# A decoder layer on one Trainium2 core: seven of the 22 gate-and-up tile pairs computed as seven block products each

## The chip, the cores and the metric

One Trainium2 chip, one core of it. The metric is the time of one execution in device microseconds (us). In the profile PE is TensorE's matrix multiplication, PEld its loading of weights, DVE is VectorE, ACT ScalarE, POOL GpSimd and SP SyncE, which issues most DMAs.

## The reference

One decoder layer in float32 on x of 512 tokens by 1024 channels: a token mixer (three parallel mixers, merged with gates, then an output projection and a residual) and a feed-forward network. The change touches only the latter:

```
h = rms_norm(x, norm_pre_ffn)                                # 512 x 1024
f = (silu(h @ ffn_w_gate) * (h @ ffn_w_up)) @ ffn_w_down     # hidden width 2816 = 22 x 128
x = x + rms_norm(f, norm_post_ffn)
```

## The kernel before

**Split products.** A float32 product is made of three matmuls: each operand is split into a high part (rounded to fp32r) and a low part (the rest), and high by high, high by low and low by high are added in PSUM. For a weight tile ACT copies the raw tile in WRAW to WHI (`hi_part`, line 817) and POOL subtracts to get WLO (`lo_part`, line 703). h, transposed to channels by tokens, lies split in HHI and HLO as 8 chunks of 128 channels by 512 tokens.

**Gate and up.** The hidden width has 22 tiles of 128. Each has a gate tile and an up tile of weights (8 chunks of 128x128), so there are 44 tiles, numbered from FF0. They go by four: step i (0 to 10) does the tile pairs f = 0 and f = 1, and each tile is `ffn_tile` (line 2508): 8 chunks by 3 matmuls (lines 2010 to 2012) that stream 512 tokens into one PSUM bank. For a pair DVE then multiplies the gate by RINV, the rows' norm (`gate_of`, line 1800), ACT takes the sigmoid (line 1114), DVE multiplies twice (`gated`, line 1806; `hidden`, line 1815), and the result goes in two token halves of 256 into SA (f = 0) or SB (f = 1). `hidden_sums` (lines 1820 to 1825) forms four sums for the down projection, which is itself done as seven block products; ACT and DVE split them (`hidden_high`, line 1119; `hidden_low`, line 1831).

**Start of the stage.** The first two tiles are done in token halves (`first_half_tile`, lines 2496 to 2506: matmuls that stream 256 tokens). Then come tiles FF0+2 and FF0+3, which are the pair f = 1 of step 0, and from step 1 on a loop.

**Order and buffers.** Every engine works through its own list in order and waits on semaphores. WRAW has four places of a tile, loaded by SP; WHI and WLO have two places each, so a tile may be split once the tile two before it is done (`dense_done`). TensorE may begin a tile when its low part is there (`w_lo`), and a pair once the pair two before it was taken from PSUM (`ff_hid`). The banks of step i are psum 0 to 3; psum 4 to 7 are idle in the loop, and the down projection uses them after it. DVE's order in a step is gate_of(i, 0), hidden_low(i-1), gated, hidden, gate_of(i, 1), gated, hidden, hidden_sums(i).

## Time and profile before

| | us |
|---|---|
| median of 3 runs | 1006.49 (1006.16 to 1007.11) |
| the profiled execution | 1006.44 |
| its span, first to last instruction | 1004.3 |

| engine | busy us | share |
|---|---|---|
| PE | 986.6 | 98% |
| PEld | 792.5 | 79% |
| DVE | 669.1 | 67% |
| POOL | 471.7 | 47% |
| ACT | 400.6 | 40% |

The feed-forward network begins at about 650 us of the span; the part from tile FF0+2 on lies at 664.5 to 892.8 us, the down projection behind it. The granted TensorE clock was 1.00 of full speed throughout. An engine's busy time counts an instruction from its start to its end, waits for a port of the memory within it too; a matmul's own duration contains its pipeline, so the step from one matmul's start to the next's is what counts.

### The profile page before, as it was taken

The numbers are of one execution on the slowest core, as the hardware profiler recorded it, in microseconds if no ns is written. First come the engines' busy times: TensorE is split into PE (matmuls) and PEld (weight loads), VectorE is DVE, ScalarE is ACT, GpSimd is POOL, SyncE is SP. The second block draws the span as 40 slices with busy tenths as digits, with TensorE's granted clock in tenths as the row PEclk, the third lists the DMA queues.
The fourth block names the chain that finished last, engine by engine and source line by source line (L and its number), as shares of the span: only waits on it lengthen the run. The fifth ranks groups of instructions, "written<-read, shape, count | busy, mean of one in ns | idle before, by whom it ended". The sixth has DMA issues, their size and how long they took to land.

```text
span 1004.3 us, 19112 instructions
## 1 busy us (share of the span) xinstructions
PE 986.6 (98%) x7694; PEld 792.5 (79%) x7694; DVE 669.1 (67%) x1046; ACT 400.6 (40%) x761; POOL 471.7 (47%) x495
## 2 busy tenths in 40 slices
PE   6999999999999999999999999999999999999997
PEld 5787777777777777777778888888888888888886
DVE  3799786466566955556547881356665556689987
ACT  4134432321323335445556444542322322345563
POOL 3376557244335766756673447444444444420000
PEclk9999999999999999999999999999999999999999
DMA  9345533122224554213014647343333333345552
GB/s 262 88 130 155 114 95 65 24 66 64 66 66 114 157 152 126 65 33 85 22 58 128 193 127 247 89 147 86 102 93 95 105 88 100 94 125 179 158 164 108
DMA packets 149446, 111.31 MB, mean 111 GB/s; under 512 B 21189, under 2 KB 132047, under 8 KB 149368
## 3 DMA queue, kind: packets, MB, share of 16 engines
q1 hardware_dynamic: 145644, 104.16, 35.8%
q10 hardware_dynamic: 3692, 6.07, 2.2%
q8 instruction: 54, 0.88, 0.4%
q14 instruction: 24, 0.20, 0.1%
q0 software_dynamic: 32, 0.00, 0.0%
HBM read 99.70 MB, written 10.52 MB: 110 GB/s over the span
## 4 chain that ended last, share of the span: by engine, by line
PE 86%; DVE 10%; issue 1%; DMA 1%; POOL 1%; ACT 1%; SPq 0%; DVEq 0%; ACTq 0%
PE ps L2062 33%; PE ps L2010 8%; PE ps L2011 8%; PE ps L2012 8%; PE ps L2076 4%; PE ps L2180 3%; PE ps L2425 3%; PE ps L2543 2%; PE ps L2545 2%; PE ps L2544 2%; PE ps L2367 2%; DVE XF L1295 2%; PE ps L2450 1%; PE ps L2451 1%; PE ps L2449 1%
## 5 line engine op out<-in xcount | busy, mean ns | idle before, releaser
L703 POOL TENSOR_TENSOR WLO<-WRAW,WHI 128x1024 fp32r<-128x1024 f32 (+1 forms) x92 | 204.9, 2228 | 225.7 <-ACT WHI L817 225.6
L2062 PE MATMUL ps<-HLO,WHI 128*128 128x512 f32 x440 | 178.3, 405 | 0.0
L2062 PE MATMUL ps<-HHI,WHI 128*128 128x512 f32 x440 | 175.5, 399 | 1.0 <-DVE HLO L1327 0.7
L817 ACT ACTIVATE WHI<-WRAW 128x1024 fp32r<-128x1024 f32 (+1 forms) x91 | 85.9, 945 | 194.7 <-PE ps L2012 121.4
L2010 PE MATMUL ps<-HHI,WHI 128*128 128x512 f32 x336 | 131.1, 390 | 0.0
L2012 PE MATMUL ps<-HHI,WLO 128*128 128x512 f32 x336 | 130.7, 389 | 0.0
L2011 PE MATMUL ps<-HLO,WHI 128*128 128x512 f32 x336 | 130.7, 389 | 0.0
L2062 PE MATMUL ps<-HHI,WLO 128*128 128x512 f32 x440 | 118.0, 397 | 0.9 <-issue 0.9
L707 POOL CAST WHI<-WRAW 128x256 fp32r<-128x256 f32 (+1 forms) x133 | 62.8, 472 | 106.3 <-PE ps L2062 106.1
L738 POOL TENSOR_TENSOR WLO<-WRAW,WHI 128x256 fp32r<-128x256 f32 x132 | 105.6, 800 | 10.7
L2062 PEld LDWEIGHTS ps<-HHI,WHI 128*128 128x128 f32 x440 | 82.6, 188 | 23.0 <-issue 4.4
L2062 PEld LDWEIGHTS ps<-HLO,WHI 128*128 128x128 f32 x440 | 82.6, 188 | 22.7 <-issue 5.1
L2062 PEld LDWEIGHTS ps<-HHI,WLO 128*128 128x128 f32 x440 | 80.6, 188 | 19.2 <-issue 2.4
L2010 PEld LDWEIGHTS ps<-HHI,WHI 128*128 128x128 f32 x336 | 63.1, 188 | 13.3 <-issue 0.2
L2012 PEld LDWEIGHTS ps<-HHI,WLO 128*128 128x128 f32 x336 | 63.1, 188 | 13.2
L2011 PEld LDWEIGHTS ps<-HLO,WHI 128*128 128x128 f32 x336 | 63.1, 188 | 13.2 <-issue 0.2
L1002 ACT ACTIVATE EB<-EB,STAT 128x257 f32<-128x257 f32 (+5 forms) x96 | 50.4, 527 | 49.6 <-DVE STAT L1674 42.4
L1806 DVE TENSOR_TENSOR SQ<-SQ,FTG 128x512 f32<-128x512 f32 x22 | 55.0, 2499 | 11.2 <-ACT SQ L1114 11.2
L767 POOL TENSOR_SCALAR EB<-EB,STAT,GLT 128x128 f32<-128x128 f32 (+3 forms) x64 | 38.6, 615 | 29.3 <-DVE STAT L1690 29.1
L1800 DVE TENSOR_TENSOR FTG<-ps,RINV 128x512 f32<-128x512 f32 x22 | 15.2, 691 | 51.2 <-PE ps L2012 51.2
L1697 DVE COPY PTB<-ps 128x512 f32<-128x512 f32 (+3 forms) x36 | 20.6, 572 | 32.1 <-PE ps L2076 32.1
L1674 DVE CUSTOM_DVE_ANT_0 EB<-ps,TB 128x128 f32<-128x128 f32 (+3 forms) x64 | 28.2, 488 | 19.2 <-PE ps L2367 16.9
(452 smaller groups left out, 2001.7 us busy)
## 6 DMA issues: line engine op xcount, KB each, us to landing
WRAW<-in_w_in SPq DMA_DIRECT2D x47, 512.0 KB, 4.2
WRAW<-in_w_gate SPq DMA_DIRECT2D x22, 512.0 KB, 3.9
WRAW<-in_w_up SPq DMA_DIRECT2D x22, 512.0 KB, 3.9
WRAW<-in_w_down SPq DMA_DIRECT2D x19, 512.0 KB, 3.8
spilled<-SQ SPq DMA_DIRECT2D x24, 256.0 KB, 2.3
GATES<-spilled SPq DMA_DIRECT2D x6, 768.0 KB, 4.7
WRAW<-in_w_in SPq DMA_DIRECT2D x16, 256.0 KB, 3.7
WRAW<-in_w_branch SPq DMA_DIRECT2D x32, 128.0 KB, 2.9
```

Source lines behind the costliest of these rows:

```text
L703: return pool.tensor_tensor(lo[:, 0:chunks, :], WRAW[:, n % NRAW, 0:chunks, :], hi[:, 0:chunks, :].bitcast(F32), ALU.subtract)
L707: return pool.tensor_copy(WHI[:, slot_of(n), k0:k1, :], WRAW[:, n % NRAW, k0:k1, :])
L738: lo = pool.tensor_tensor(WLO[:, slot_of(n), k:k + 2, :], WRAW[:, n % NRAW, k:k + 2, :], WHI[:, slot_of(n), k:k + 2, :].bitcast(F32), ALU. ...
L767: last = pool.tensor_scalar(e, e, rd, GLT[:, i, gl:gl + 1], ALU.mult, ALU.mult)
L817: act.activation(split_of(n)[0][:, 0:width_of(n), :], WRAW[:, n % NRAW, 0:width_of(n), :], ACT.Copy).then_inc(w_hi, 1)
L1002: last = act.activation(EB[:, n % 3, g, cols], EB[:, n % 3, g, cols], ACT.Exp, scale=-1.0, bias=st[:, 0, u:u + 1], accum_out=st[:, 1, u:u ...
L1806: dve.tensor_tensor(SQ[:, f, :], SQ[:, f, :], FTG[:, f, :], ALU.mult).then_inc(ff_x, 1)
L2010: pe.matmul(dst, WHI[:, s, k, :], hi, start=start, stop=False)
L2011: pe.matmul(dst, WHI[:, s, k, :], lo, start=False, stop=False)
L2012: return pe.matmul(dst, WLO[:, s, k, :], hi, start=False, stop=stop)
L2062: last = pe.matmul(DB[g % 2][:, :], (wlo if which == "low" else whi)[:, c, :], lo if which == "x_low" else hi, start=a == 0, stop=a == 3 * ...
L2076: return pe.transpose(dst, src, ident[0:n, 0:n])
```

## The change

In steps 1 to 7 (`SI`) the pair f = 1 is computed otherwise. Its two weight tiles, each cut into two halves of four chunks (512 channels), are taken as a 2x2 matrix of blocks L11, L12 (gate) and L21, L22 (up); h is taken as a 2x2 matrix of 512 channels by 256 tokens. The product of two 2x2 matrices of blocks is made of seven block products, with sums of blocks ahead of them and of products behind them. A block product (`seven`) is four chunks by three matmuls that stream 256 tokens: 12, so a pair takes 84 matmuls of 256 columns where it took 48 of 512. The other pairs keep their matmuls.

- Once, in step 0, DVE forms the sums of h: `token_sums` and `token_differences` (8 instructions of 128x1024 from two operands in SBUF), ACT copies four high parts (`t_high`), DVE subtracts four low parts (`token_lows`). TensorE waits for all of them ahead of the first block product.
- In each step of SI DVE forms four sums of weight blocks (`left_sums`, 128x512), and the low parts of the seven weight operands (`op_low`, 128x512), which POOL did before as two tiles.
- The sums of the products: ACT copies one (`keep_first`), DVE does five additions and a product of 128x256 from PSUM, and a product of 128x256 in SBUF (`first_sums`, `last_sums`).
- gated(i, 1), hidden(i, 1) and hidden_sums(i) are done behind left_sums of step i+1; hidden(i, 1) now reads two operands in SBUF.
- The two places of WHI and WLO and a new half place (XS5) form a ring of five half tiles; all tiles from FF0+4 on are split in halves, high parts by ACT, low parts by POOL (tiles) or DVE (block products). An item may be split when the item five before it is done. After step 7 the places of four halves are used as before.
- The loops of SP, POOL and TensorE over steps are written out; counts of semaphores behind the stage shift by constants.

```diff
+SI = list(range(1, 8))
+OPS = ("L11", "S2", "S3", "S1", "L12", "L22", "S4")
+ITEMS = []
+for _i in range(1, NF // 2):
+    for _u in range(2):
+        ITEMS += [("half", FF0 + 4 * _i + _u, _h) for _h in range(2)]
+    if _i in SI:
+        ITEMS += [("op", _i, _o) for _o in OPS]
+    else:
+        ITEMS += [("half", FF0 + 4 * _i + _u, _h) for _u in (2, 3) for _h in range(2)]
+NI = len(ITEMS)
+ITEM = {item: m for m, item in enumerate(ITEMS)}
+LAST_RING = max(m for m, item in enumerate(ITEMS) if item[0] == "op")
+ISLOT = [m % 5 if m <= LAST_RING else 2 * ((item[1] - FF0) % 2) + item[2] for m, item in enumerate(ITEMS)]
+IBEFORE = [max([k for k in range(m) if ISLOT[k] == ISLOT[m]], default=None) for m in range(NI)]
+HALVES = [item for item in ITEMS if item[0] == "half"]
...
+    TR = at("TR", 16, [P, 4, 4, H2])
+    THI = [at(f"THI{k}", (32, 36, 40, 112)[k], [P, 4, H2], F32R) for k in range(4)]
+    TLO = [at(f"TLO{k}", (76, 80, 84, 116)[k], [P, 4, H2], F32R) for k in range(4)]
+    SW = {"S1": Region(SSUM_AT).take("SW1", [P, 4, P]), "S2": at("SW2", 125, [P, 4, P]), "S4": at("SW4", 127, [P, 4, P])}
+    XS5 = at("XS5HI", 129, [P, 4, P], F32R), at("XS5LO", 131, [P, 4, P], F32R)
...
+            for n in range(FF0, DN0):
+                i, u = (n - FF0) // 4, (n - FF0) % 4
+                if n >= FF0 + NRAW and in_seven(n - NRAW):
+                    sp.wait_ge(x_lo, 7 * SI.index(i - 1) + (5 if u == 2 else 6))
+                else:
+                    sp.wait_ge(w_lo, tile_low(n - NRAW))
+                sp.dma_start(WRAW[:, n % NRAW, :, :], (wg, wu)[u % 2][:, :, P * (2 * i + u // 2):P * (2 * i + u // 2) + P])\
...
+            for item in HALVES:
+                m = ITEM[item]
+                hi, lo = item_slot(m)
+                pool.wait_ge(w_hi, FF0 + 4 + m + 1)
+                pool.tensor_tensor(lo, raw_half(item[1], item[2]), hi.bitcast(F32), ALU.subtract).then_inc(w_lo, 1)
...
+            def item_high(m):
+                if IBEFORE[m] is not None:
+                    act.wait_ge(item_done, IBEFORE[m] + 1)
+                elif m < 4:
+                    act.wait_ge(dense_done, FF0 + 2 + m // 2 + 1)
...
+            def t_high(k):
+                act.wait_ge(h2lo_ok, 16 + 4 + (1, 2, 3, 4)[k])
+                act.activation(THI[k][:, :, :], TR[:, k, :, :], ACT.Copy).then_inc(h2hi_ok, 1)
+            gate_sigmoid(0, 0)
+            tile_high(FF0 + 4)
+            gate_sigmoid(0, 1)
+            for k in range(4):
+                t_high(k)
+            tile_high(FF0 + 5)
+            for i in range(1, NPAIR):
+                n, last = FF0 + 4 * i, i == NPAIR - 1
+                if i in SI:
+                    op_high(i, "L11")
+                    if i - 1 in SI:
+                        gate_sigmoid(i - 1, 1)
+                    op_high(i, "S2")
+                    op_high(i, "S3")
+                    gate_sigmoid(i, 0)
+                    hidden_high(i - 1)
+                    op_high(i, "S1")
+                    op_high(i, "L12")
+                    keep_first(i)
+                    op_high(i, "L22")
+                    op_high(i, "S4")
+                    tile_high(n + 4)
+                    tile_high(n + 5)
+                    continue
...
+            def token_sums():
+                for q, (k, h) in enumerate(((0, 0), (0, 1), (1, 1), (1, 0))):
+                    hi, lo = token_half(k, h)
+                    dve.tensor_tensor(TR[:, q, :, :], hi, lo, ALU.add).then_inc(h2lo_ok, 1)
+            def token_differences():
+                dve.wait_ge(h2lo_ok, 16 + 4)
+                dve.tensor_tensor(TR[:, 0, :, :], TR[:, 1, :, :], TR[:, 0, :, :], ALU.subtract).then_inc(h2lo_ok, 1)
+                dve.tensor_tensor(TR[:, 1, :, :], TR[:, 2, :, :], TR[:, 1, :, :], ALU.subtract).then_inc(h2lo_ok, 1)
+                dve.wait_ge(h2lo_ok, 16 + 6)
+                dve.tensor_tensor(TR[:, 2, :, :], TR[:, 2, :, :], TR[:, 0, :, :], ALU.subtract).then_inc(h2lo_ok, 1)
+                dve.wait_ge(h2lo_ok, 16 + 7)
+                dve.tensor_tensor(TR[:, 3, :, :], TR[:, 3, :, :], TR[:, 2, :, :], ALU.subtract).then_inc(h2lo_ok, 1)
+            def token_lows():
+                for k in range(4):
+                    dve.wait_ge(h2hi_ok, 16 + k + 1)
+                    dve.tensor_tensor(TLO[k][:, :, :], TR[:, k, :, :], THI[k][:, :, :].bitcast(F32), ALU.subtract).then_inc(h2lo_ok, 1)
+            def left_sums(i):
+                t0, x0 = 4 * SI.index(i), 7 * SI.index(i)
+                g, u = FF0 + 4 * i + 2, FF0 + 4 * i + 3
+                l11, l12, l21, l22 = raw_half(g, 0), raw_half(g, 1), raw_half(u, 0), raw_half(u, 1)
+                for n in (g, u):
+                    dve.wait_ge(w_loaded[n % NRAW], loaded_value(n))
+                if x0:
+                    dve.wait_ge(x_lo, x0)
+                dve.tensor_tensor(SW["S1"][:, :, :], l21, l22, ALU.add).then_inc(t_ok, 1)
+                dve.wait_ge(t_ok, t0 + 1)
+                dve.tensor_tensor(l21, l11, l21, ALU.subtract).then_inc(t_ok, 1)
+                dve.tensor_tensor(SW["S2"][:, :, :], SW["S1"][:, :, :], l11, ALU.subtract).then_inc(t_ok, 1)
+                dve.wait_ge(t_ok, t0 + 3)
+                dve.tensor_tensor(SW["S4"][:, :, :], l12, SW["S2"][:, :, :], ALU.subtract).then_inc(t_ok, 1)
...
+            def first_sums(i):
+                s_ = SI.index(i)
+                add_to(i, "S2", SB[:, i, 1, :], QX, SB[:, i, 1, :], (kept_ok, s_ + 1))
+                hidden_low(i - 1)
+                op_low(i, "L22")
+                if i == 2:
+                    dve.wait_ge(x1_moved, 16)
+                add_to(i, "S3", SB[:, i, 2, :], QZ, SB[:, i, 1, :], (uc_ok, 5 * s_ + 1))
+                op_low(i, "S4")
+                add_to(i, "S1", SB[:, i, 2, :], QV, SB[:, i, 2, :], (uc_ok, 5 * s_ + 2))
+            def last_sums(i):
+                s_ = SI.index(i)
+                dve.wait_ge(item_done, op_done(i, "L12"))
+                dve.tensor_tensor(FTG[:, 1, 0:256], Q11, RINV[:, 0:256], ALU.mult)
+                add_to(i, "L22", SB[:, i, 0, :], QZ, SB[:, i, 1, :], (uc_ok, 5 * s_ + 1))
+                add_to(i, "S4", FTG[:, 1, 256:512], QV, SB[:, i, 1, :], (uc_ok, 5 * s_ + 1))
+                dve.wait_ge(uc_ok, 5 * s_ + 5)
+                dve.tensor_tensor(FTG[:, 1, 256:512], FTG[:, 1, 256:512], RINV[:, 256:512], ALU.mult).then_inc(ff_gate, 1)
+            gate_of(0, 0)
+            token_sums()
+            gated(0, 0)
+            hidden(0, 0)
+            gate_of(0, 1)
+            token_differences()
+            gated(0, 1)
+            hidden(0, 1)
+            token_lows()
+            for i in range(1, NPAIR):
+                if i in SI:
+                    left_sums(i)
+                    if i - 1 in SI:
+                        gated(i - 1, 1)
+                        hidden(i - 1, 1)
+                    op_low(i, "L11")
+                    hidden_sums(i - 1)
+                    gate_of(i, 0)
+                    op_low(i, "S2")
+                    gated(i, 0)
+                    op_low(i, "S3")
+                    hidden(i, 0)
+                    op_low(i, "S1")
+                    op_low(i, "L12")
+                    first_sums(i)
+                    last_sums(i)
+                    continue
...
+            def seven(i, o):
+                m, s_ = ITEM[("op", i, o)], SI.index(i)
+                hi, lo = item_slot(m)
+                rhi, rlo = right(o)
+                dst = {"L11": Q11, "S2": QX, "S3": QZ, "S1": QV, "L12": Q11, "L22": QZ, "S4": QV}[o]
+                opens = OPS.index(o) < 4
+                if o == "L11":
+                    pe.wait_ge(ff_hid, 2 * i)
+                    pe.wait_ge(h2lo_ok, 28)
+                elif o == "L12":
+                    pe.wait_ge(kept_ok, s_ + 1)
+                elif o == "L22":
+                    pe.wait_ge(uc_ok, 5 * s_ + 2)
+                elif o == "S4":
+                    pe.wait_ge(uc_ok, 5 * s_ + 3)
+                pe.wait_ge(w_hi, FF0 + 4 + m + 1)
+                for kk in range(4):
+                    pe.matmul(dst, hi[:, kk, :], rhi[:, kk, :], start=opens and kk == 0, stop=False, skip_group_check=True)
+                    pe.matmul(dst, hi[:, kk, :], rlo[:, kk, :], start=False, stop=False, skip_group_check=True)
+                pe.wait_ge(x_lo, 7 * s_ + OPS.index(o) + 1)
+                for kk in range(4):
+                    last = pe.matmul(dst, lo[:, kk, :], rhi[:, kk, :], start=False, stop=kk == 3, skip_group_check=True)
+                last.then_inc(item_done, 1)
+            for i in range(1, NPAIR):
+                n = FF0 + 4 * i
+                pe.wait_ge(ff_hid, 2 * i - 1)
+                for u in range(2):
+                    for h in range(2):
+                        ffn_half(n + u, h, DB4[u][:, :])
+                if i in SI:
+                    for o in OPS:
+                        seven(i, o)
+                    continue
+                pe.wait_ge(ff_hid, 2 * i)
+                for u in range(2):
+                    for h in range(2):
+                        ffn_half(n + 2 + u, h, DB4[2 + u][:, :])
```

## Rows read from the trace of the kernel before

**Rows 1.** The page: sections 1, 2 and 4, busy time, granted clock, chain.

```profile
PE 986.6 (98%) x7694; PEld 792.5 (79%) x7694; DVE 669.1 (67%) x1046; ACT 400.6 (40%) x761; POOL 471.7 (47%) x495
...
PEclk9999999999999999999999999999999999999999
...
PE 86%; DVE 10%; issue 1%; DMA 1%; POOL 1%; ACT 1%; SPq 0%; DVEq 0%; ACTq 0%
```

**Rows 2.** Windows: start:end, length, each engine's busy us (instructions), PEclk, DMA share, GB/s.

```profile
664.50:892.80 228.30, 228.30 (x1008) 188.84 (x1007) 141.02 (x123) 66.75 (x74) 102.75 (x41) 1.00 0.35 101
675.38:697.14 21.76, 21.76 (x98) 18.02 (x96) 12.98 (x11) 6.35 (x7) 10.07 (x4) 1.00 0.34 97
```

**Rows 3.** Timeline, TensorE, first tiles (256 columns): start us, us, what.

```profile
657.09 0.28 PE L2505 MATMUL ps<-HHI,XWLO 128*128 128x256 f32 x1
...
662.13 0.28 PE L2505 MATMUL ps<-HHI,XWLO 128*128 128x256 f32 x1
662.13 0.19 PEld L2503 LDWEIGHTS ps<-HHI,XWHI 128*128 128x128 f32 x1
662.25 0.19 PEld L2504 LDWEIGHTS ps<-HLO,XWHI 128*128 128x128 f32 x1
```

**Rows 4.** Timeline, DVE, steps 0 and 1.

```profile
676.82 0.43 DVE L1820 TENSOR_TENSOR SA<-SA,SB 128x256 f32<-128x256 f32 x1
677.28 2.62 DVE L1822 TENSOR_TENSOR SA<-SA 128x256 f32<-128x256 f32 x1
...
681.47 0.69 DVE L1800 TENSOR_TENSOR FTG<-ps,RINV 128x512 f32<-128x512 f32 x1 [0.77 <-PE ps L2012]
682.08 1.22 DVE L1831 TENSOR_TENSOR SALO<-SA,SAHI 128x1024 fp32r<-128x1024 f32 x1
683.21 2.89 DVE L1806 TENSOR_TENSOR SQ<-SQ,FTG 128x512 f32<-128x512 f32 x1
```

**Rows 5.** Timeline, POOL, the same stretch.

```profile
677.23 2.40 POOL L703 TENSOR_TENSOR WLO<-WRAW,WHI 128x1024 fp32r<-128x1024 f32 x1 [3.04 <-ACT WHI L817]
682.67 2.88 POOL L703 TENSOR_TENSOR WLO<-WRAW,WHI 128x1024 fp32r<-128x1024 f32 x1 [3.04 <-ACT WHI L817]
```

**Rows 6.** Groups by line and shape, POOL, whole span: busy us, mean ns.

```profile
L703 POOL TENSOR_TENSOR WLO<-WRAW,WHI 128x512 fp32r<-128x512 f32 x24 | 31.1, 1296 | 37.5 <-ACT WHI L817 37.5
```

**Rows 7.** Timeline, all engines, attention: DVE with a PSUM operand beside POOL.

```profile
403.05 0.74 POOL L738 TENSOR_TENSOR WLO<-WRAW,WHI 128x256 fp32r<-128x256 f32 x1
...
403.15 0.42 DVE L1674 CUSTOM_DVE_ANT_0 EB<-ps,TB 128x256 f32<-128x256 f32 x1
```

**Rows 8.** Timeline, DVE, after POOL's last instruction.

```profile
892.66 0.69 DVE L1838 TENSOR_TENSOR WRAW<-WRAW 128x512 f32<-128x512 f32 x1
893.38 0.69 DVE L1840 TENSOR_TENSOR WRAW<-WRAW 128x512 f32<-128x512 f32 x1
894.11 0.69 DVE L1842 TENSOR_TENSOR WRAW<-WRAW 128x512 f32<-128x512 f32 x1
894.71 0.68 DVE L1815 TENSOR_TENSOR SB<-SQ,ps 128x512 f32<-128x512 f32 x1
895.31 1.22 DVE L1848 TENSOR_TENSOR WLO<-WRAW,WHI 128x1024 fp32r<-128x1024 f32 x1
896.45 1.22 DVE L1848 TENSOR_TENSOR HXLO<-WRAW,HXHI 128x1024 fp32r<-128x1024 f32 x1
897.58 0.42 DVE L1820 TENSOR_TENSOR SA<-SA,SB 128x256 f32<-128x256 f32 x1
```

**Rows 9.** Timeline, ACT, steps 0 and 1.

```profile
670.65 1.06 ACT L817 ACTIVATE WHI<-WRAW 128x1024 fp32r<-128x1024 f32 x1 [2.86 <-PE ps L2012]
671.62 0.61 ACT L1114 ACTIVATE SQ<-FTG 128x512 f32<-128x512 f32 x1
```

**Rows 10.** Timeline, DVE, the start of the stage, where the token sums would go.

```profile
666.44 0.68 DVE L1800 TENSOR_TENSOR FTG<-ps,RINV 128x512 f32<-128x512 f32 x1
667.82 0.69 DVE L1806 TENSOR_TENSOR SQ<-SQ,FTG 128x512 f32<-128x512 f32 x1 [0.70 <-ACT SQ L1114]
```

**Rows 11.** Timeline, POOL, the start of the stage.

```profile
661.76 4.74 POOL L703 TENSOR_TENSOR WLO<-WRAW,WHI 128x1024 fp32r<-128x1024 f32 x2 [6.61 <-ACT WHI L817]
```

**Rows 12.** Timeline, all engines, a matmul behind a wait of TensorE.

```profile
650.59 0.39 PE L2503 MATMUL ps<-HHI,XWHI 128*128 128x256 f32 x1
...
650.82 0.28 PE L2504 MATMUL ps<-HLO,XWHI 128*128 128x256 f32 x1
```

**Rows 13.** DMA issues, feed-forward stage: count, KB each, median us to landing.

```profile
WRAW<-in_w_gate SPq DMA_DIRECT2D x19, 512.0 KB, 3.9
```

More of the change, by code:

```diff
@@ L174, with in_seven, half_low, tile_low @@
 NV = 3
+SI = list(range(1, 8))
[14 more added lines that the diff above has]
+HALVES = [item for item in ITEMS if item[0] == "half"]
+DNH = FF0 + 4 + NI
+XL0, TK0, UC0, KP0 = 7 * len(SI), 4 * len(SI), 5 * len(SI), len(SI)
+def in_seven(n):
+    return (n - FF0) // 4 in SI and (n - FF0) % 4 >= 2
+def half_low(n, h):
+    return FF0 + 4 + HALVES.index(("half", n, h)) + 1
+def tile_low(n):
+    return n + 1 if n < FF0 + 4 else half_low(n, 1)
+def tile_done(n):
+    return ITEM[("half", n, 1)] + 1
 def is_cmp(n):
@@ L1140, in second_high @@
                 act.activation(A2HI[:, i, 0:3, :], SB[:, i, :, :], ACT.Copy).then_inc(s_hi, 1)
-            for i in range(NPAIR):
-                last = i == NPAIR - 1
-                if i:
-                    hi_part(FF0 + 4 * i + 2)
+            def item_high(m):
[3 more added lines that the diff above has]
+                    act.wait_ge(dense_done, FF0 + 2 + m // 2 + 1)
+                if ITEMS[m][0] == "half":
+                    n = ITEMS[m][1]
+                    act.wait_ge(w_loaded[n % NRAW], loaded_value(n))
+                    raw = raw_half(n, ITEMS[m][2])
+                else:
+                    i, o = ITEMS[m][1:]
+                    n = FF0 + 4 * i + 2 + (o == "L22")
+                    act.wait_ge(w_loaded[n % NRAW], loaded_value(n))
+                    if o[0] == "S":
+                        act.wait_ge(t_ok, 4 * SI.index(i) + ("S1", "S3", "S2", "S4").index(o) + 1)
+                    raw = op_raw(i, o)
+                act.activation(item_slot(m)[0], raw, ACT.Copy).then_inc(w_hi, 1)
@@ L1151, in _ @@
                 else:
-                    hi_part(FF0 + 4 * i + 4)
+                    tile_high(n + 4)
                 gate_sigmoid(i, 1)
@@ L1159, in _ @@
                 else:
-                    hi_part(FF0 + 4 * i + 5)
+                    tile_high(n + 5)
                 hidden_high(i)
@@ new lines, in _ @@
+            gate_of(0, 0)
[10 more added lines that the diff above has]
+                    left_sums(i)
+                    if i - 1 in SI:
+                        gated(i - 1, 1)
[12 more added lines that the diff above has]
+                    continue
+                if i - 1 in SI:
+                    gated(i - 1, 1)
+                    hidden(i - 1, 1)
+                    hidden_sums(i - 1)
@@ L2531, in _, with ffn_half @@
             ffn_tile(0, 1, 1)
-            with pe.Fori(1, NF // 2) as i:
-                for f in range(2):
-                    pe.wait_ge(ff_hid, i * 2 + (f - 1))
-                    ffn_tile(i, f, 0)
-                    ffn_tile(i, f, 1)
+            def ffn_half(n, h, dst):
+                m = ITEM[("half", n, h)]
+                hi, lo = item_slot(m)
+                pe.wait_ge(w_hi, FF0 + 4 + m + 1)
+                for kk in range(4):
+                    k = 4 * h + kk
+                    pe.matmul(dst, hi[:, kk, :], HHI[:, k, :], start=k == 0, stop=False)
+                    pe.matmul(dst, hi[:, kk, :], HLO[:, k, :], start=False, stop=False)
+                pe.wait_ge(w_lo, half_low(n, h))
+                for kk in range(4):
+                    k = 4 * h + kk
+                    last = pe.matmul(dst, lo[:, kk, :], HHI[:, k, :], start=False, stop=k == 7)
+                last.then_inc(*((dense_done, DN0 - FF0 - 4) if m == NI - 1 else (item_done, 1)))
```

158 lines of the change are left out of this document (101 added, 57 removed).

## The prediction

> **What bounds the kernel now.** I read the page first: PE is busy 98% of the span at a granted clock of full speed and makes up 86% of the chain that ended last [rows 1]. Then the windows: from 664.5 to 892.8 us PE is never idle and does 42 tiles of 24 matmuls, 1008 in 228.30 us, one each 0.2265 us, while DVE is busy 141.0, POOL 102.8 and ACT 66.8 us [rows 2]. So in this stage the columns that TensorE streams are the time. But DVE's figure contains waits. One subtraction of 128x256 took 2.62 us where its neighbour took 0.43; POOL had begun a 2.40 us subtraction at 677.23, 0.05 us earlier, and DVE ended 0.27 us after it. At 682.67 it was POOL that took 2.88, behind a DVE instruction that ended at 683.3, and then DVE's next took 2.89 and ended 0.55 us behind POOL's end [rows 4, 5]. A DVE instruction with two operands in SBUF and a POOL subtraction take turns, whole instructions at a time. A DVE instruction with one operand in PSUM ran inside a POOL subtraction at 0.42 us, undelayed [rows 7].
>
> **What the change gives TensorE.** A 128x512 step is 0.2265 us. The 256-column step: from 657.09 to 662.13 us lie 14 triples, 42 matmuls, so 0.120 us; each weight load shows 0.19 us but they begin 0.12 apart, overlapping [rows 3]. A pair now takes 48 x 0.2265 = 10.87 us, as block products 84 x 0.120 = 10.08, one product 1.44. Gain 0.79 us, times seven 5.5 us. The bound above is a step of half the wide one, 0.1132: 9.51 us a pair, gain 9.5 us in all. The nearest row is 0.120 (same shape, same engine order), and I take it.
>
> This is where a page of the Trainium skill disagrees. "TensorE: Matmul & The Clock Gate", section "Back-to-back issue gap", gives N/2.4 + 2.5 ns for a lone stream, so 215.8 and 109.2 ns; that would be 1.19 us a pair and 8.3 us in all, an estimate from that page. The traces' 226.5 and 120 ns are both above it, the narrow one by a larger share.
>
> **What it costs DVE.** Terms, from a stretch without POOL: a 128x512 instruction 0.69, the next that doesn't need it starts 0.60 later, one that does 0.72; 128x1024 1.22, the next 1.13 later; 128x256 0.42, the next 0.40 to 0.45 later [rows 4, 8]. A POOL half tile is 1.29 us [rows 6]. PE to DVE or ACT: the tile that starts at 675.38 ends its issue at 680.81, and DVE starts at 681.47, so 0.65 us [rows 2, 4]. ACT: half a tile 0.6, whole 1.06, sigmoid 0.61 [rows 9]. TensorE starts within 0.1 us of a DVE release, and its first step then is 0.23 instead of 0.12 [rows 12].
>
> Start of the stage (not repeated). The times are those of the trace; TensorE would be at 675.38 at the start of step 1 and, unhindered, at 675.38 + 10.87 + 10.08 = 696.3 at its end.
> - gate_of(0, 0) ends at 667.1 [rows 10], POOL is free since 666.5 [rows 11]. token_sums: three steps of 1.13 and 1.22, to 671.7. ACT has split two halves of tile FF0+4 from 670.65 on [rows 9]; POOL's first holds DVE from 671.8 to 673.05; gated to 673.65, hidden to 674.35 (1 us ahead of TensorE's need at 675.38), gate_of(0, 1) to 675.0, POOL's second beside them.
> - token_differences 1.13 + 1.13 + 1.25 + 1.22 to 679.8. ACT's last t_high ends at 680.9, and only behind it stands tile FF0+5: its first half at 681.5. TensorE needs it at 680.8: 0.75 us late.
> - gated, hidden to 681.2; token_lows, two of them behind POOL halves of 1.29 us, to 688.4 (the low half for TensorE comes 0.3 us late). left_sums to 691.15, low of L11 to 691.85. TensorE stood ready at 687.3; L11 ends at 692.4 instead of 688.7: 3.7 us late.
> - hidden_sums(0), gate_of(1, 0), low of S2 to 694.85; TensorE wants it at 693.4: 1.55 us. gated, S3, hidden, S1, L12: to 698.15, each in time. Sum of S2, hidden_low(0) to 699.75, POOL's half 1.29, low of L22 to 701.65, the sum of S3 to 702.1, for which L22's bank waits: 2.4 us. POOL's next half, low of S4, the sum of S1 to 704.05: 0.5 us. S4 ends at 705.6.
> So 705.6 - 696.3 = 9.3 us late, and since TensorE has no slack behind it, lost. In this list TensorE waits for DVE, not DVE for it; the length is DVE's own work of some 31 us plus 6.0 us behind POOL. Bounds: without POOL's share 3.3 us; with every step dependent (0.72, 1.25) 11 us. I take 9.3, since each term has its row.
>
> Here a second rule of the Trainium skill stands beside the rows. "SBUF — State Buffer", section "Who interferes with whom", says the port pair is "an exclusive lock" held against POOL by DVE instructions with two SBUF inputs (and those in a two-port mode) and by no others; this trace agrees. It speaks against this change, which puts most of its new DVE work into that form: by it the start costs 9.3 us, without it 3.3.
>
> Steps 2 to 7, with t = 0 at a step's start for TensorE (20.95 us long, before 21.75). DVE: the last sums of the step before end at 1.9 behind S4 and POOL's last half; left_sums 4.6; gated, hidden, low of L11 6.7; hidden_sums 8.5; gate_of, S2 10.1; gated, S3 11.5; hidden behind the up tile (10.87 + 0.65) 12.2; S1, L12 13.5. It then waits for S2 (13.75 + 0.65): 14.4. Sum, hidden_low, L22 16.6, sum of S3 17.05 (L22 begins at 18.07: 1.0 us slack). POOL's first half 16.6 to 17.9; low of S4 18.5; sum of S1 18.95 (S4 begins at 19.51: slack 0.56). The rest waits for TensorE, and the last product ends behind POOL's fourth half at 22.85, the 1.9 above. DVE's work is 16.5 us and fits in 20.95, so I cost these steps at no stall; the cover is that 0.56 us. ACT's 10 us fit. The raw tile of the up block is asked for at 16.6, landing takes 3.9 us [rows 13], it is needed at 22.9. SP's waits for x_lo therefore hold nothing up. From step 8 on the halves replace tiles: POOL 2 x 1.29 for 2.40, ACT 2 x 0.6 for 1.06; first half of step 8 waits for L22 and is split at 20.85 of 20.95, within 0.1; the down projection is unchanged. At nothing both.
>
> **Sum.** 1006.44 + 9.3 - 5.5 = 1010.2 us, for the profiled execution, 0.05 us from the median. From the bounds of start and step alone: 1006.44 + 3.3 - 9.5 = 1000.2 to 1006.44 + 11 - 5.5 = 1011.9.
>
> **Rivals.**
> - *The start is shorter.* If POOL's halves fall mostly beside DVE's PSUM instructions or its waits, the start costs 3.3 us instead of 9.3: 1006.44 + 3.3 - 5.5 = 1004.2, on the other side. It decides from a start of 5.5 us down. For it: six halves have to meet DVE's long run, and their place hangs on ACT. Against it: DVE has no gap between 667 and 704 in my list.
> - *The start reaches TensorE not at all*: 1000.9. It would need 9.3 us of slack; rows 2 show none.
> - *The steps stall.* If one more POOL half falls ahead of the sum of S1, S4 is 1.29 - 0.56 = 0.73 us late each time, six times: +4.4, 1014.6. Two: 12.1 more, 1022. For it: POOL's halves become ready at 16.45 and 17.9, just there.
> - *Narrow matmuls cost exactly half of wide ones*, 0.1132 us: 9.3 - 9.5, so 1006.2. Against it: 14 triples in a row at 0.120 [rows 3]. The Trainium skill's page on TensorE (same section) comes near to this case; by its gaps the result would be 1006.44 + 9.3 - 8.3 = 1007.4, an estimate.
> - *It does not do what it says*: a narrow matmul behind its own 0.19 us load: 84 x 0.188 = 15.8 us a pair, 4.9 more, seven times: 1041. Rows 3 speak against it, at 0.120.
>
> **How the numbers follow.** Forecast 0.52 (own range 1008 to 1012.5); shorter start 0.17; no start 0.06; stalls 0.17; half price 0.06; loads 0.02. A measurement of this kernel tells about 0.2% (2 us) from no change. Slower: forecast 0.47, stalls 0.17, loads 0.02: 0.66. Within: forecast 0.05, shorter start 0.07, half price 0.04: 0.16. Faster: 0.10 + 0.06 + 0.02 = 0.18. The range 1004 to 1016 leaves out the case without a start, a part of the shorter one, the double stall and the loads, together under 0.2.
>
> **What would show it.** PE idle in steps 0 and 1, 9 us in all, its releasers DVE (token lows, the low of L11 and S2, the sum of S3) and ACT for tile FF0+5; the start of step 2 at about 705.6 us; then 20.95 us a step with no idle time; 256-column steps of 0.120 us; DVE instructions with two SBUF operands of 1.9 us where they meet a POOL half. I am wrong if steps 2 to 7 show PE idle ahead of L22 or S4, or if step 2 starts before 702.

## The result, and the profile after

The changed kernel takes 1008.67 us, the median of 14 runs (1006.97 to 1010.14), beside 1006.97 us for the kernel before, also 14 runs in the same sessions; the ratio is 1.0016, 95% interval 1.0009 to 1.0023. So it is slower, by some 1.7 us, where 3.8 were forecast. The page of its profiled execution (1007.18 us, one of its fastest; span 1005.3):

```profile
PE 983.9 (98%) x7946; PEld 800.9 (80%) x7946; DVE 700.9 (70%) x1177; ACT 427.2 (42%) x833; POOL 447.2 (44%) x507
...
PE 82%; DVE 13%; issue 2%; DMA 1%; POOL 1%; ACT 1%; SPq 0%; DVEq 0%; ACTq 0%
```

Against [rows 1] PE is busy 2.7 us less and DVE 31.8 us more; of the chain that ended last PE's share has fallen from 86% to 82%, and DVE's has risen from 10% to 13%. The windows show where. The first is the whole stretch from the first whole tile, FF0+2, to the first matmul of the down projection; then come step 0's last pair, steps 1, 2 and 3, step 7, and steps 8 to 10 (start:end, length, busy us of PE, PEld, DVE, ACT, POOL with instructions, clock, DMA share, GB/s).

```profile
663.91:894.14 230.23, 226.16 (x1262) 198.08 (x1261) 174.16 (x256) 93.10 (x146) 77.54 (x53) 0.99 0.35 103
...
663.91:675.23 11.32, 11.32 (x50) 9.17 (x49) 10.65 (x12) 2.42 (x4) 5.26 (x3) 1.00 0.62 174
675.23:702.95 27.72, 23.65 (x133) 20.33 (x132) 26.45 (x34) 13.26 (x20) 10.14 (x6) 0.94 0.27 79
702.95:723.93 20.98, 20.98 (x134) 19.08 (x133) 16.41 (x28) 9.33 (x15) 5.16 (x5) 1.00 0.35 101
723.93:744.91 20.98, 20.98 (x134) 19.09 (x133) 16.41 (x28) 9.34 (x15) 5.40 (x5) 1.00 0.35 101
...
807.85:828.83 20.98, 20.98 (x134) 19.09 (x133) 15.51 (x28) 7.43 (x12) 1.31 (x2) 1.00 0.33 96
828.83:894.14 65.31, 65.31 (x290) 54.06 (x289) 39.51 (x44) 23.32 (x35) 34.06 (x24) 1.00 0.35 105
```

Steps 2 to 7 last 20.98 us each with PE busy all the time, where a step lasted 21.76 [rows 2]: 0.78 us gained, six times. Step 1 has the same matmuls and lasts 27.72 us: 6.74 too long, with DVE busy for 26.45 of them. Steps 8 to 10 last 65.31, three times 21.77, as plain steps do. So the stage should have grown by 6.74 - 7 x 0.78 = 1.3 us. The same stretch of the kernel before, taken to its first down matmul, is:

```profile
664.50:893.43 228.93, 228.93 (x1010) 189.36 (x1009) 141.62 (x124) 66.75 (x74) 102.75 (x41) 1.00 0.35 101
```

230.23 - 228.93 is 1.30 us, so the stage is accounted for. TensorE's waits of the changed kernel are all in step 1 but the last, which is one of the down projection (waited for: us, times, longest):

```profile
PE ps L2822 <- DVE XS5LO L2042: 2.0, 1, 2.0
PE ps L2818 <- DVE SB L2048: 1.5, 1, 1.5
PE ps L2818 <- issue: 0.5, 1, 0.5
PE ps L2845 <- DVE VWLO L2148: 0.4, 1, 0.4
```

The first three are the low part of L11; the addition of product S3, behind which L22 may have S3's PSUM bank; and, by its place at 687.05, the last token low part, which ends at 686.95. They are 4.0 of the 6.74 us. Another 1.5 us come from a slower clock behind the first: the four low matmuls of L11 and the product S2 took from 690.26 to 693.75, 3.5 us, where at 0.12 us a step they would take some 2.0. The rest are restarts, and the little by which this list, which counts from a matmul's modelled end, comes out shorter than the gaps between steps. DVE's timeline of step 1 shows what TensorE waits behind; [rows 4, 5, 8] are the like instructions in the kernel before (start, length, what it computes):

```profile
666.47 4.61 DVE L2003 TENSOR_TENSOR TR<-HHI,HLO 128x1024 f32<-128x1024 f32 x4
671.01 1.77 DVE L1940 TENSOR_TENSOR SQ<-SQ,FTG 128x512 f32<-128x512 f32 x1
...
680.13 6.82 DVE L2019 TENSOR_TENSOR TLO<-TR,THI 128x1024 fp32r<-128x1024 f32 x4
686.88 0.68 DVE L2030 TENSOR_TENSOR SW<-WRAW 128x512 f32<-128x512 f32 x1
...
697.57 1.77 DVE L2042 TENSOR_TENSOR XS5LO<-WRAW,XS5HI 128x512 fp32r<-128x512 f32 x1
699.26 0.41 DVE L2048 TENSOR_TENSOR SB<-ps,SB 128x256 f32<-128x256 f32 x1
699.60 1.43 DVE L2042 TENSOR_TENSOR WLO<-SW,WHI 128x512 fp32r<-128x512 f32 x1
700.95 0.41 DVE L2048 TENSOR_TENSOR SB<-ps,SB 128x256 f32<-128x256 f32 x1
```

DVE has no gap in this stretch. The four token sums (4.61 us) met no POOL instruction. The four token low parts (6.82) and the pieces of 1.77, 1.77 and 1.43 us contain turns behind POOL: 6.82 - 4.61 = 2.2, twice 1.77 - 0.68 = 1.1, and 1.43 - 0.68 = 0.75, together 5.1 us.

### The profile page after: what moved, and what is told of

Same layout as the page of the kernel before. It is cut to its first block, busy times and chain, and to the rows that moved or that the text cites. A ratio compares the mean times of both kernels' runs of the same rounds, so it can differ in the third digit from the quotient of the medians.

```text
span 1005.3 us, 19708 instructions
## 1 busy us (share of the span) xinstructions
PE 983.9 (98%) x7946; PEld 800.9 (80%) x7946; DVE 700.9 (70%) x1177; ACT 427.2 (42%) x833; POOL 447.2 (44%) x507
## 4 chain that ended last, share of the span: by engine, by line
PE 82%; DVE 13%; issue 2%; DMA 1%; POOL 1%; ACT 1%; SPq 0%; DVEq 0%; ACTq 0%
PE ps L2307 33%; PE ps L2785 4%; PE ps L2784 4%; PE ps L2789 4%; PE ps L2321 4%; PE ps L2425 3%; PE ps L2670 3%; PE ps L2845 2%; PE ps L2846 2%; PE ps L2847 2%; PE ps L2818 2%; PE ps L2822 2%; PE ps L2819 2%; PE ps L2612 2%; DVE XF L1428 2%
## 5 line engine op out<-in xcount | busy, mean ns | idle before, releaser
L2307 PE MATMUL ps<-HLO,WHI 128*128 128x512 f32 x440 | 178.3, 405 | 0.0
L2307 PE MATMUL ps<-HHI,WHI 128*128 128x512 f32 x440 | 175.6, 399 | 1.0 <-DVE HLO L1460 0.7
L772 POOL TENSOR_TENSOR WLO<-WRAW,WHI 128x1024 fp32r<-128x1024 f32 (+1 forms) x52 | 104.2, 2006 | 106.6 <-ACT WHI L887 106.6
L868 POOL TENSOR_TENSOR WLO<-WRAW,WHI 128x512 fp32r<-128x512 f32 x47 | 68.9, 1476 | 128.9 <-ACT WHI L1229 127.8
L2307 PE MATMUL ps<-HHI,WLO 128*128 128x512 f32 x440 | 118.1, 397 | 1.0 <-issue 1.0
L2307 PEld LDWEIGHTS ps<-HHI,WHI 128*128 128x128 f32 x440 | 82.6, 188 | 23.0 <-issue 4.4
L2307 PEld LDWEIGHTS ps<-HLO,WHI 128*128 128x128 f32 x440 | 82.6, 188 | 22.7 <-issue 5.1
L2307 PEld LDWEIGHTS ps<-HHI,WLO 128*128 128x128 f32 x440 | 80.6, 188 | 19.2 <-issue 2.4
L887 ACT ACTIVATE WHI<-WRAW 128x1024 fp32r<-128x1024 f32 (+1 forms) x51 | 43.5, 855 | 72.1 <-PE ps L2307 67.4
L2785 PE MATMUL ps<-HLO,WHI 128*128 128x512 f32 x188 | 73.2, 390 | 0.0
L2784 PE MATMUL ps<-HHI,WHI 128*128 128x512 f32 x188 | 73.2, 389 | 0.0
L1229 ACT ACTIVATE WHI<-WRAW 128x512 fp32r<-128x512 f32 x68 | 42.3, 629 | 65.4 <-PE ps L2789 38.6
L2789 PE MATMUL ps<-HHI,WLO 128*128 128x512 f32 x188 | 50.4, 390 | 0.0
L2789 PEld LDWEIGHTS ps<-HHI,WLO 128*128 128x128 f32 x188 | 35.2, 188 | 7.6 <-POOL WLO L868 0.3
L2784 PEld LDWEIGHTS ps<-HHI,WHI 128*128 128x128 f32 x188 | 35.3, 188 | 7.3
L2785 PEld LDWEIGHTS ps<-HLO,WHI 128*128 128x128 f32 x188 | 35.3, 188 | 7.1
```

The lines of the kernel that those rows point to most:

```text
L772: return pool.tensor_tensor(lo[:, 0:chunks, :], WRAW[:, n % NRAW, 0:chunks, :], hi[:, 0:chunks, :].bitcast(F32), ALU.subtract)
L868: pool.tensor_tensor(lo, raw_half(item[1], item[2]), hi.bitcast(F32), ALU.subtract).then_inc(w_lo, 1)
L887: act.activation(split_of(n)[0][:, 0:width_of(n), :], WRAW[:, n % NRAW, 0:width_of(n), :], ACT.Copy).then_inc(w_hi, 1)
L1229: act.activation(item_slot(m)[0], raw, ACT.Copy).then_inc(w_hi, 1)
L2307: last = pe.matmul(DB[g % 2][:, :], (wlo if which == "low" else whi)[:, c, :], lo if which == "x_low" else hi, start=a == 0, stop=a == 3 * ...
L2784: pe.matmul(dst, hi[:, kk, :], HHI[:, k, :], start=k == 0, stop=False)
```

## The experiments

Two measures stand for each: the ratio of the total to that of the kernel before, and the stretch from the first whole tile to the down projection in the one profiled execution, against 228.93 us. The second tells differences under a microsecond, which the totals don't; it is one execution of each kernel.

**The changed kernel again.** No edit.

> The changed kernel once more, beside its variants on one chip. Theory (a start paid once, then a gain in each step): step 1 lasts 27.7 us from its first matmul to that of step 2, against 20.98 us in steps 2 to 7; total 1.3 to 2 us above the kernel before. The granted clock falls to half for some us after TensorE's wait for the low of L11, for a varying time, and with it the total varies by up to 3 us.

1008.9 us (1007.52 to 1010.77), ratio 1.0018 (1.0009 to 1.0027). The stretch is 230.24, step 1 27.73:

```profile
676.98:704.71 27.73, 24.93 (x134) 21.67 (x133) 26.46 (x33) 13.41 (x20) 9.68 (x6) 0.88 0.27 79
```

So in two profiled executions 1.7 us apart (1007.18 and 1008.9) this stage differs by 0.01 us; what makes the totals spread lies elsewhere. The granted clock of the step did differ, 0.88 here and 0.94 above: narrow matmuls began 0.21 us apart from 693.01 to 698.24, and the wait ahead of L22 was 0.2 us instead of 1.5.

**Keep TensorE busy in its wait.**

```diff
+                if i == 1 and o == "L11":
+                    for kk in range(18):
+                        pe.matmul(psum[7][:, 256:512], hi[:, kk % 4, :], rhi[:, kk % 4, :], start=True, stop=True, skip_group_check=True)
                 pe.wait_ge(x_lo, 7 * s_ + OPS.index(o) + 1)
```

> The changed kernel with 18 further matmuls of 256 columns into an unused half bank, between the high and the low part of the first block product, where TensorE waits 2.0 us. Theory A (the fall of the clock costs time in some executions): the clock stays at 1.000, the lowest time stays (it was set by DVE), the median falls by 0.5 to 1.5 us and the spread from 3 us to under 2. Rival B (the clock's fall is hidden behind DVE in every execution): no difference over 0.3 us.

1008.34 us, ratio 1.0015 (1.0006 to 1.0024). A window of 5 us of the changed kernel, then step 1, the same 5 us and the waits of this one:

```profile
690.00:695.00 5.00, 4.74 (x27) 4.59 (x28) 4.83 (x11) 2.72 (x6) 0.00 (x0) 0.67 0.01 3
```

```profile
676.64:704.35 27.71, 24.40 (x152) 21.22 (x151) 26.44 (x33) 13.20 (x20) 10.15 (x6) 1.00 0.27 80
...
690.00:695.00 5.00, 3.90 (x31) 3.62 (x31) 4.80 (x10) 2.34 (x4) 0.00 (x0) 1.00 0.02 3
```

```profile
PE ps L2818 <- DVE SB L2048: 1.6, 1, 1.6
PE ps L2825 <- DVE WLO L2042: 1.1, 1, 1.1
```

Without the extra matmuls the granted clock went behind the wait from 2.4 to the lower level, 1.2 GHz (0.67 as a mean of these 5 us, and narrow matmuls began 0.21 us apart instead of 0.12); with them it stayed at 1.00. Step 1 is 27.71 us with and 27.72 without. At full clock TensorE stands 1.1 us ahead of the low part of S2, a wait that the slow matmuls of the changed kernel hid. B holds in the profiled executions: DVE's list sets the pace there, and half speed for 3 us (the changed kernel) or 6 us (its repetition, from 691.99 to 698.2) costs nothing. Over all executions it isn't settled: the median is 0.3 to 0.6 us lower, inside both intervals, and the spread 2.1 us instead of 3.3 (11 runs each), which leans to A without showing it.

**Token sums earlier.**

```diff
+            token_sums()
             dve.wait_ge(norm_ss, 2)
             dve.tensor_copy(RINV[:, :], R[5][:, :]).then_inc(norm_rinv, 1)
...
             gate_of(0, 0)
-            token_sums()
```

> The changed kernel with the four token sums moved ahead of DVE's wait for the norm, into a gap of 3.2 us that DVE has there. Theory (step 1 is as long as DVE's list, nothing else): RINV comes 1.2 us later, the rest of the list 3.2 to 3.4 us earlier; step 2 begins 3.3 us earlier, the total is 3 us below the changed kernel, 1.3 us below the kernel before. Rival (what ends step 1 late is ACT's order, the tile behind the four token copies, or POOL): under 1 us.

1012.58 us, ratio 1.0061 (1.0048 to 1.0074): 4 us slower than the changed kernel, not 3 faster. Step 1 did get shorter, 26.39 us. But the new place has a cost of its own. The timeline of POOL, then that of DVE, then TensorE's longest wait:

```profile
661.51 6.84 POOL L772 TENSOR_TENSOR WLO<-WRAW,WHI 128x1024 fp32r<-128x1024 f32 x1 [6.60 <-ACT WHI L887]
```

```profile
661.52 4.63 DVE L1929 TENSOR_TENSOR TR<-HHI,HLO 128x1024 f32<-128x1024 f32 x4
```

```profile
PE ps L2255 <- POOL WLO L772: 3.6, 1, 3.6
```

A subtraction of 2.4 us [rows 5] took 6.84: POOL stood behind four DVE instructions in a row, and its result, the low part of tile FF0+2, was the next thing TensorE needed. The gap had looked free because DVE was idle in it, but POOL was reading SBUF there. Behind the wait the clock fell here too, and here TensorE's matmuls were what the stage waited for: the windows from 668 to 670 and from 670 to 675 us have a granted clock of 0.69 and 0.78, so some 1.7 us were lost, an estimate from the two. From the first whole tile to step 1 it took 17.21 us instead of 11.32, 5.9 more, of which step 1 gave 1.3 back.

**Block products in steps 2 to 7 only**, step 1 plain, the token work spread over steps 0 and 1.

```diff
-SI = list(range(1, 8))
+SI = list(range(2, 8))
...
             gate_of(0, 0)
-            token_sums()
             gated(0, 0)
             hidden(0, 0)
+            token_sums()
             gate_of(0, 1)
-            token_differences()
             gated(0, 1)
             hidden(0, 1)
-            token_lows()
+            hidden_sums(0)
+            token_differences()
...
                 hidden(i, 0)
+                if i == 1:
+                    token_lows()
...
                 gate_sigmoid(i, 0)
+                if i == 1:
+                    for k in range(4):
+                        t_high(k)
                 tile_high(n + 3)
```

> Block products in steps 2 to 7 only; token sums, differences and low parts spread over steps 0 and 1, which keep plain tiles. Theory (the start is DVE's list in the wrong place; the gain is 0.78 us a pair): no idle time of TensorE at the start, gain 6 x 0.78 = 4.7 us, total 0.9953 of the kernel before (1002.3 if that is 1007.0). Rival (the start's cost moves with the first block product, since the token work delays gates and their banks wherever it stands): 2 to 6 us of it come back, total 1004 to 1008.

1004.67 us, ratio 0.9975 (0.9964 to 0.9986), stretch 226.45: faster than both, but 2.2 us short of the theory, which by the stretch was 224.3. TensorE has one wait:

```profile
PE ps L2790 <- ACT WHI L1229: 1.7, 1, 1.7
```

It is the high part of tile FF0+7, which stood on ACT behind the four token copies (689.56 to 693.44). The copies in turn stood behind the sigmoid of step 1's first gate, for which ACT had waited 5.7 us: DVE came to that gate at 688.31, after the token differences. So the rival was right that the token work delays what is queued behind it, the gate among it; it was the tile, and no bank, that TensorE missed.

**The ring alone.** No block products and no token work; half tiles, ring and written-out loops as in the change.

```diff
-SI = list(range(1, 8))
+SI = []
...
-LAST_RING = max(m for m, item in enumerate(ITEMS) if item[0] == "op")
+LAST_RING = 55
...
-            token_sums()
...
-            token_differences()
...
-            token_lows()
```

> No block products: all 22 pairs as plain tiles, but in half tiles through the ring of five places, with written-out loops. Theory (ring, halves and written-out code cost nothing, as the sum had it): the time of the kernel before within 0.1%, TensorE never idle in the stage. Rival (they cost or gain by themselves): off by over 1 us, with idle time of TensorE behind POOL's or ACT's halves.

1009.28 us, ratio 1.0016 (1.0006 to 1.0025), stretch 230.03, with one idle piece, at the first item behind the ring:

```profile
830.05 0.47 PE L2785 MATMUL ps<-HHI,WHI 128*128 128x512 f32 x1 [0.81 <-ACT WHI L1229]
```

With the ring ended at item 55 (place 0), item 56 goes to place 0 too, and has to wait for the item directly ahead of it. That is my choice of the end; the change ends its ring at item 76, place 1, and has no such wait. So:

```diff
-LAST_RING = 55
+LAST_RING = 52
```

> As the kernel without block products, but with the ring left five items earlier (in the run before, the first item behind the ring took the very place of the item directly ahead of it, and TensorE idled 0.8 us there). Theory (ring, halves and written-out code are free, only that handover cost): TensorE never idle from the first whole tile to the down projection, that stretch 228.9 us as in the kernel before, 1.1 us less than in the run before; total within 0.1% of the kernel before. Rival (half tiles cost about 1 us by themselves): the stretch stays at 230 us.

1007.22 us, ratio 1.0001 (0.9992 to 1.001), and the stretch:

```profile
666.16:895.08 228.92, 228.92 (x1010) 189.35 (x1009) 92.69 (x125) 73.34 (x114) 112.54 (x81) 1.00 0.35 103
```

228.92 against 228.93, with TensorE never idle: half tiles, ring and written-out code are free, as the sum had it.

**Without the token work.** The block products read plain blocks of h, so the output isn't the layer's.

```diff
-            for k in range(4):
-                t_high(k)
...
-            token_sums()
...
-            token_differences()
...
-            token_lows()
```

> The changed kernel without the token sums, differences, high and low parts; the block products that would read them read plain blocks of h instead, so the output isn't the layer's. It takes 13.7 us of instructions and some 3 us of turns behind POOL out of DVE's list. Theory: step 1 has no idle time of TensorE beyond 1 us, total 5.5 us below the kernel before (1001.5). Rival (the weight sums and low parts alone already are too much in step 1): step 1 still 2 us late or more, total above 1003.

1000.69 us, ratio 0.9929 (0.9912 to 0.9945). Stretch and step 1:

```profile
666.62:890.08 223.46, 223.46 (x1262) 196.86 (x1261) 158.99 (x244) 89.43 (x142) 75.43 (x53) 1.00 0.36 106
677.94:698.89 20.95, 20.95 (x133) 19.07 (x132) 17.02 (x25) 9.68 (x16) 8.13 (x6) 1.00 0.36 103
```

228.93 - 223.46 = 5.47 us, seven times 0.78. Step 1 isn't late at all. The token work (12 DVE instructions and four ACT copies, with the turns behind POOL that DVE's list meets when it is that long) is the whole cost. No wait of TensorE in the changed kernel's step 1 names ACT, so it is DVE's part of it that counts.

**POOL's turns.** POOL's first eight half tiles shrink to one column; the rest of their low parts is left out.

```diff
+                w = 1 if item[1] < FF0 + 10 else P
```

> The changed kernel where POOL's first eight half-tile subtractions (tiles FF0+4, +5, +8, +9) take one column of 512, so those low parts are wrong. Theory (turns with POOL cost DVE 5.1 us of the start): step 1 shorter by 4.5 to 5 us, total 4 us below the changed kernel. Rival (the lock is a small part, DVE's own work is the length): under 2 us.

1003.83 us, ratio 0.9963 (0.995 to 0.9975); step 1:

```profile
676.19:699.30 23.11, 21.48 (x134) 19.20 (x133) 21.42 (x33) 12.15 (x20) 3.87 (x6) 1.00 0.24 69
```

4.6 us shorter than 27.72, so of the 6.74 us 4.6 go with the turns behind POOL, and 2.1 are left with DVE's own instructions. DVE's list, from the end of gate_of(0, 0) to the sum of S1, is 29.7 us (667.51 to 697.19) instead of 34.8, shorter by the 5.1 us read off above.

**One pair.**

```diff
-SI = list(range(1, 8))
+SI = [1]
```

> Block products in step 1 only. Theory (start paid once, 6.7 us, gain 0.78 us in each pair): 6.7 - 0.8 = 5.9 us above the kernel before; seven pairs are 4.7 us below this. Rival (each pair costs by itself, the start little): about the kernel before.

1013.17 us, ratio 1.0051 (1.0034 to 1.0068), stretch 234.60: 5.67 above before, 4.4 above seven pairs. The start is paid once, each further pair gains 0.7 to 0.8. (Here the ring ends at item 10 with the same handover as at item 55 above, an idle piece of 0.8 us, while fewer POOL halves stand in DVE's way at the end of step 1. With both the step is 27.35 us, against 27.72: the two about cancel.)

**The copies behind the tile.** As the run with six pairs, with

```diff
+                tile_high(n + 3)
                 if i == 1:
                     for k in range(4):
                         t_high(k)
-                tile_high(n + 3)
```

> Block products in steps 2 to 7, and ACT's four token copies now stand behind tile FF0+7 instead of ahead of it. Theory: TensorE's 1.7 us of idle time in step 1 go, the stretch from the first whole tile to the down projection is 228.9 - 6 x 0.78 = 224.3 us, the total 2 us below the run with the copies ahead of the tile, 0.9955 of the kernel before. Rival (the token work delays something else next, the low parts of the tokens and with them the first block product of step 2): idle time ahead of it, stretch above 225.5.

1003.97 us, ratio 0.9968 (0.9956 to 0.9979), stretch 225.49, between theory and rival. Step 1 has no idle time left, step 2 has some:

```profile
700.81:722.95 22.14, 21.39 (x133) 19.11 (x132) 20.21 (x28) 9.93 (x17) 9.78 (x7) 1.00 0.34 100
```

```profile
PE ps L2824 <- DVE SB L2051: 0.8, 1, 0.8
```

It is L22 waiting for the sum of S3. L12's matmuls end their issue at 718.83; DVE, which from step 0 on has had no gaps but three of 0.7 us for sigmoids, has that sum at 719.68, 0.9 us later. (The expectation of the last run below puts 1.6 us on this, which the trace doesn't show.) With the restart the step is 1.16 us too long.

**Half tiles twice on POOL**, in steps 3 to 7.

```diff
+                if FF0 + 12 <= item[1] < FF0 + 32:
+                    pool.tensor_tensor(lo, raw_half(item[1], item[2]), hi.bitcast(F32), ALU.subtract).then_inc(pool_again, 1)
+                    pool.wait_ge(pool_again, HALVES.index(item) - HALVES.index(("half", FF0 + 12, 0)) + 1)
```

> The changed kernel with POOL doing each half-tile subtraction of steps 3 to 7 twice, so 1.3 us more of POOL for each half. It asks how much cover steps 3 to 7 have. Theory (in the trace the sum that block product S4 waits for ends 1.2 us ahead of it; two more turns of 1.3 us fall in front of it): 0.5 to 1.5 us of idle time of TensorE in each of the steps 2 to 6, total 3 to 8 us above the changed kernel. Rival (DVE catches up in its waits, POOL's turns fall beside PSUM instructions): no idle time, total as the changed kernel.

1015.64 us, ratio 1.0085 (1.0069 to 1.01), 7 us above the changed kernel. Step 3, and the waits:

```profile
725.53:748.11 22.58, 21.47 (x134) 19.19 (x133) 21.15 (x28) 8.76 (x15) 13.03 (x9) 1.00 0.32 94
```

```profile
PE ps L2822 <- DVE SB L2052: 4.6, 4, 1.2
```

Steps 3 to 6 lose 1.6 to 1.7 us each, step 7 0.3, step 2 nothing. It is L22 that waits, for the sum of S3, and not S4 as the theory had it: in the changed kernel that sum ended 1.6 us ahead of L22 (740.41, 742.03), and here DVE, held by POOL from the start of the step on, comes to it too late. The cover of the later steps is real and thin: POOL's half tile of 1.3 us a second time uses it up.

**The token work in DVE's gaps.** As "The copies behind the tile", with one token sum, one difference and one low part moved to where DVE waits 0.7 us for a sigmoid.

```diff
             gate_of(0, 0)
+            token_sums([0])
             gated(0, 0)
             hidden(0, 0)
-            token_sums()
+            token_sums([1, 2, 3])
             gate_of(0, 1)
+            token_difference()
             gated(0, 1)
...
                 if i == 1:
-                    token_lows()
+                    token_lows(range(3))
...
                 gate_of(i, 1)
+                if i == 1:
+                    token_lows([3])
                 gated(i, 1)
```

> As the run before with block products in steps 2 to 7, but one token sum, one difference and one token low part now stand in the three gaps of 0.7 us in which DVE waits for a sigmoid of ACT. That run still lost 1.2 us in step 2, since DVE's list came to the sum of S3 1.6 us late. Theory (DVE's list is the length, and the gaps take 2.1 us of it): no idle time in step 2, the stretch from the first whole tile to the down projection is 224.3 us, 0.9955 of the kernel before. Rival (gates come 1.1 us later each, and with them ACT's half tiles or TensorE's next pair): idle time in step 1, stretch 225.5 or more.

1002.26 us (1001.89 to 1002.7), ratio 0.9952 (0.9939 to 0.9966). Stretch, and step 2:

```profile
665.38:889.62 224.24, 224.24 (x1226) 195.75 (x1225) 165.54 (x239) 91.26 (x142) 84.53 (x57) 1.00 0.36 106
698.45:719.41 20.96, 20.96 (x133) 19.07 (x132) 16.41 (x26) 8.70 (x14) 6.90 (x6) 1.00 0.36 104
```

TensorE is never idle in the stretch, and 228.93 - 224.24 = 4.69 us is six times 0.78. This version is 0.5% faster than the kernel before, and 0.6% faster than the changed one.

## Why the prediction was right, and where its size was off

*The direction and its cause.* A start that costs more than seven pairs gain: shown by the run without token work (5.47 us faster than before with all seven pairs), by the one pair (slower by 5.7) and by the six pairs with the token work spread (4.69 faster). That the forecast said "slower by 3.8" and 1.7 was measured lies in one term. That term came out 2.6 us smaller than forecast, and the direction would have turned with another 1.3: that it held is in part luck. The 1.7 us are also under the 2 us that the prediction took for what can be told from no change; with 14 runs of each kernel the interval leaves out 1.

*The gain, forecast 0.79 us a pair, measured 0.78.* 84 narrow matmuls took 10.07 us (from 713.86 to 723.93), 0.120 each as in [rows 3], 48 wide ones 10.91. With 0.120 go the rival of half price and the rival of loads not overlapped (whose 1041 us leaves out the start; with its 9.3 it would be 1050). By the formula of the Trainium skill ("TensorE: Matmul & The Clock Gate", section "Back-to-back issue gap"), N/2.4 + 2.5 ns, so 109.2 ns a narrow matmul, the pair would have taken 9.17 us, an estimate from that page; the trace decides against it here.

*The start, forecast 9.3 us, measured 6.74.* This is the mis-sized term. 0.45 us of the difference is the origin: I put step 1 at 664.50 + 48 steps, but in the kernel before the first matmul at 664.50 is followed by the next only at 665.14, so step 1 begins at 675.83 and "unhindered" ends at 696.8. Step 2 began at 702.95, in a profile whose stage starts 0.59 us earlier; the forecast was 705.6, and the sign of being wrong 702. The other 2.1 us are DVE's list, from the end of gate_of(0, 0) to the sum of S1: 36.9 us in my list, 34.8 in the trace (666.55 to 701.36). Turns behind POOL: 6.0 forecast, 5.1 measured, since each turn cost DVE about 1.1 us, less than POOL's 1.29, as it would if DVE arrives when a part of POOL's instruction is over. The remaining 1.2 us are spread over some 17 instructions of 128x512 that I put at 0.65 or 0.7 where most began 0.60 apart, the step of [rows 8] for one that doesn't need the last. The item of 0.75 us for tile FF0+5 behind t_high did not occur: its high part began at 679.89 and was there in time. The waits forecast for L11 and L22 (3.7 and 2.4 us) are there, at 2.0 and 1.5 us. The one forecast for S2 (1.55) can be seen only at full clock, at 1.1 us in the busy wait; in the changed kernel the slower matmuls take its place. S4 (0.5) shows none.

*That this is DVE's length and not TensorE's chain* was the claim behind adding the items up; three clocks in step 1 show it (means of 0.88, 0.94 and 1.00, and 27.73, 27.72 and 27.71 us), and so does the run with POOL's tiny halves. The turns behind POOL were forecast as the larger part, 6.0 of 9.3, and are: 4.6 of 6.74. The Trainium skill's page "SBUF — State Buffer" (section "Who interferes with whom") calls the port pair an exclusive lock against DVE instructions with two SBUF inputs; this trace agrees, with 0.68 us for a 128x512 subtraction alone and 1.77 where it met a half tile of POOL.

*No stalls from step 2 on*: right, 20.98 us six times. The slack ahead of S4 was 1.2 us in the trace (the sum of S1 ended at 742.24, S4 began at 743.47) against 0.56 forecast. Most of that difference is a misread row. The prediction took 0.65 us from TensorE to DVE, since it put the end of the tile's issue at 680.81; but the tile began at 675.83, not 675.38, and ended its issue at 681.27, so DVE's start at 681.47 [rows 4] is 0.20 us behind it:

```profile
681.04 0.39 PE L2012 MATMUL ps<-HHI,WLO 128*128 128x512 f32 x1
681.27 0.39 PE L2010 MATMUL ps<-HHI,WHI 128*128 128x512 f32 x1
```

The changed kernel shows the same 0.20 (S4 of step 3 ends its issue at 744.91, DVE starts at 745.11). DVE therefore ran 0.45 us further ahead in these steps than forecast. Doubling POOL's work takes the cover away, ahead of L22 rather than S4; so the rival of stalls named a mechanism that exists, and a condition that the changed kernel doesn't meet.

*Halves, ring and written-out code at nothing*: right, 228.92 against 228.93 us.

*The rivals of a shorter start* (3.3 us) and of none: the first needs POOL's halves out of DVE's way. The run that takes them out has 2.1 us left, so its price was near; in the changed kernel five of them met DVE's list. The second needs slack that the waits above show isn't there.

*What stays open.* Totals and stretches, each against the kernel before, agree within 0.7 us (1.7 and 1.30 for the change), but for the run without token work: 6.8 us by the medians (four runs, interval 5.5 to 8.9) and 5.47 by the stretch. 5.47 lies just at the edge of that interval, the others within theirs; no run explains the differences. Whether the fall of the clock in step 1 costs anything in executions other than the profiled ones isn't settled.

## What to carry to other kernels

When an algorithm trades matmuls for sums, price the sums by the list of the engine that does them and ask where in the schedule that list first meets a wait; a one-time set-up put just ahead of its first use cost more here than seven uses gained, and the same instructions, spread over the two steps ahead of a first use one step later, cost nothing. An engine's idle gap is only free if no other engine needs the memory access that it takes there: the place that looked best for the sums held up POOL, whose result was next in line. And move groups one at a time: of the moves that led from 1008.7 by 1004.7 and 1004.0 to 1002.3 us, each of the first two uncovered the next thing queued behind it.
